# A decoder trunk in float32: the routed experts take their tokens in tiles of 96 in place of 128

## The reference

```
def swiglu(h, w1, w3, w2):
    return (jax.nn.silu(h @ w1) * (h @ w3)) @ w2

def moe_ffn(h, w_router, w1, w3, w2):
    logits = (h @ w_router).astype(jnp.float32)
    top_v, top_i = lax.top_k(logits, TOP_K)
    top_w = jax.nn.softmax(top_v, axis=-1)
    gate = jnp.sum(jax.nn.one_hot(top_i, N_EXPERTS, dtype=jnp.float32) * top_w[..., None], axis=-2).astype(h.dtype)
    y = jnp.zeros_like(h)
    for e in range(N_EXPERTS):
        y = y + gate[..., e:e + 1] * swiglu(h, w1[e], w3[e], w2[e])
    return y
```

## Time and profile before

| | |
|---|---|
| median of 3 runs | 1988.61 us (1986.09 to 1989.08) |
| profiled execution: its time | 1987.18 us |
| profiled execution: span of the core | 1985.4 us |
| TensorE busy | 1911.2 us (96%) |
| VectorE busy | 1471.9 us (74%) |
| ScalarE busy | 1150.4 us (58%) |
| read from memory | 530.83 MB |
| first and last large matmul of the experts start at | 951.35 and 1965.30 us |

### The profile page before, as it was taken

One profiled execution on the slowest core, in us unless ns is written; L12 is line 12 of the kernel. 1 busy time (PEld: TensorE's weight loads), 2 busy tenths in 40 slices (PEclk: granted clock), 3 DMA queues, 4 the chain that ended last, 5 costly groups with the idle time before them and its releaser, 6 DMA issues.

```text
span 1985.4 us, 29859 instructions
## 1 busy us (share of the span) xinstructions
PE 1911.2 (96%) x10960; PEld 1582.2 (80%) x10960; DVE 1471.9 (74%) x1503; ACT 1150.4 (58%) x1245; POOL 93.4 (5%) x134
## 2 busy tenths in 40 slices
PE   5999999999999999998999999999999999999996
PEld 4878888789987888887887787877878878778885
DVE  3755565744567655656788889888888888888888
ACT  2554554334435545542667767677677676767773
POOL 0610100000005201000000000000000000000000
PEclk9999999999999999998999999999999999999998
DMA  8846434685557544344899999999999999999993
GB/s 315 303 151 220 167 127 160 209 315 191 186 179 245 208 140 162 125 161 144 319 342 350 349 344 348 351 339 353 334 353 348 342 345 336 357 341 348 343 364 127
DMA packets 275638, 533.10 MB, mean 269 GB/s; under 512 B 10768, under 2 KB 23392, under 8 KB 275424
## 3 DMA queue, kind: packets, MB, share of 16 engines
q1 hardware_dynamic: 275552, 531.91, 75.6%
HBM read 530.83 MB, written 1.05 MB: 268 GB/s over the span
## 4 chain that ended last, share of the span: by engine, by line
PE 89%; DVE 6%; ACT 2%; issue 1%; DMA 1%; DVEq 1%; SPq 0%; ACTq 0%
PE pA L741 18%; PE pA L742 17%; PE pA L743 17%; PE pA L746 8%; PE pO L746 7%; PE pO L741 6%; PE pO L743 6%; PE pO L742 6%; PE pT L799 4%; DVE w_lo L1846 1%; ACT w_hi L1429 1%; DMA raw<-in_ffn_w 1%; PE pT L746 1%; DVE win L2083 0%; DMA x<-in_x 0%
## 5 line engine op out<-in xcount | busy, mean ns | idle before, releaser
L1891 DVE TENSOR_TENSOR wide_lo<-raw,wide_hi 128x2048 fp32r<-128x2048 f32 x336 | 761.9, 2291 | 122.0 <-ACT wide_hi L1429 102.5
L1429 ACT ACTIVATE wide_hi<-raw 128x2048 fp32r<-128x2048 f32 x336 | 644.8, 1922 | 213.1 <-PE pO L743 119.1
L1429 ACT ACTIVATE w_hi<-raw 128x1024 fp32r<-128x1024 f32 (+1 forms) x242 | 251.2, 1045 | 337.2 <-PE pA L743 234.2
L1846 DVE TENSOR_TENSOR w_lo<-raw,w_hi 128x1024 fp32r<-128x1024 f32 (+1 forms) x242 | 294.4, 1230 | 169.0 <-ACT w_hi L1429 159.9
L741 PE MATMUL pA<-wide_hi,x_lo 128*128 128x512 f32 x896 | 359.7, 401 | 1.8 <-DVE wide_lo L1891 0.6
L743 PE MATMUL pA<-wide_hi,x_hi 128*128 128x512 f32 x896 | 353.5, 395 | 0.0
L742 PE MATMUL pA<-wide_lo,x_hi 128*128 128x512 f32 x896 | 353.5, 395 | 0.0
L741 PE MATMUL pA<-w_hi,h_lo 128*128 128x512 f32 (+2 forms) x560 | 225.8, 403 | 14.7 <-DVE w_lo L1846 10.8
L742 PE MATMUL pA<-w_lo,h_hi 128*128 128x512 f32 (+2 forms) x560 | 216.7, 387 | 0.0
L743 PE MATMUL pA<-w_hi,h_hi 128*128 128x512 f32 (+2 forms) x560 | 216.6, 387 | 0.0
L741 PEld LDWEIGHTS pA<-wide_hi,x_lo 128*128 128x128 f32 x896 | 168.0, 188 | 44.7 <-issue 4.1
(11 more groups left out here) (272 smaller groups left out, 2367.9 us busy)
## 6 DMA issues: line engine op xcount, KB each, us to landing
raw<-in_moe_w SPq DMA_DIRECT2D x336, 1024.0 KB, 6.9
raw<-in_w_in SPq DMA_DIRECT2D x56, 1024.0 KB, 6.0
raw<-in_ada_w SPq DMA_DIRECT2D x48, 1024.0 KB, 6.4
raw<-in_ffn_w SPq DMA_DIRECT2D x33, 1024.0 KB, 5.0
raw<-in_w_out SPq DMA_DIRECT2D x8, 1024.0 KB, 5.0
raw<-in_cmp_k_w SPq DMA_DIRECT2D x4, 1024.0 KB, 8.2
raw<-in_cmp_v_w SPq DMA_DIRECT2D x4, 1024.0 KB, 11.6
raw<-in_w_read_nsa SPq DMA_DIRECT2D x4, 1024.0 KB, 6.0
```

Of the source, the lines that this page charges most:

```text
L1429: return nc.scalar.activation(dst, src, ACT.Copy)
L1846: V.tensor_tensor(w_lo[m][:, 0:n], raw[s][:, i * n:(i + 1) * n], w_hi[m][:, 0:n].bitcast(F32), ALU.subtract).then_inc(raw_done, 1)
L1891: V.tensor_tensor(wide_lo[m][:, :], raw[g][:, :], wide_hi[m][:, :].bitcast(F32), ALU.subtract).then_inc(raw_done, 2)
```

## The change

The experts' tokens are taken in tiles of CAP = 96 places, and there may be PASSES = 3 passes in place of 2, chosen by two comparisons in place of one. sel, x_f, x_hi, x_lo, aT_hi and aT_lo are 96 wide. The outputs of gate_up and down, a_sb and oe use 96 partitions; their 512 columns stay. The streamed weights, their splits and their transfers stay as they are within a pass. The part of SyncE's program that issues an expert pass stands there three times, the second and third under a condition.

```
...
+
+
+CAP = 96
+PASSES = -(-SEQ // CAP)
...
-        aT_hi = sb("aT_hi", [P, CK, SEQ], F32R, at=work)
-        aT_lo = sb("aT_lo", [P, CK, SEQ], F32R, at=work + 4096)
-        x_f = sb("x_f", [P, KB, P], at=work + 8192)
-        x_hi = sb("x_hi", [P, KB, P], F32R, at=work + 12288)
-        x_lo = sb("x_lo", [P, KB, P], F32R, at=work + 16384)
+        aT_hi = sb("aT_hi", [P, CK, CAP], F32R, at=work)
+        aT_lo = sb("aT_lo", [P, CK, CAP], F32R, at=work + 4096)
+        x_f = sb("x_f", [P, KB, CAP], at=work + 8192)
+        x_hi = sb("x_hi", [P, KB, CAP], F32R, at=work + 12288)
+        x_lo = sb("x_lo", [P, KB, CAP], F32R, at=work + 16384)
...
-        sel = sb("sel", [P, TT, P], at=work + 20480)
+        sel = sb("sel", [P, TT, CAP], at=work + 20480)
...
-        slot16 = sb("slot16", [P, TT, 2 * NE + 1])
-        gate16 = sb("gate16", [P, TT, 2 * NE])
+        slot16 = sb("slot16", [P, TT, PASSES * NE + 1])
+        gate16 = sb("gate16", [P, TT, PASSES * NE])
...
-                    passes = sp.value_load(flag[0:1, 0:1], min_val=1, max_val=2)
-                    with sp.If(passes > 1):
-                        experts()
+                    passes = sp.value_load(flag[0:1, 0:1], min_val=1, max_val=PASSES)
+                    for p in range(1, PASSES):
+                        with sp.If(passes > p):
+                            experts()
...
                                 for t in range(TT):
-                                    ins = mm(pA[1 + 2 * q][:, j * P:(j + 1) * P], y[:, t, k * P:(k + 1) * P], sel[:, t, :], t == 0, t == 1)
+                                    ins = mm(pA[1 + 2 * q][:, j * P:j * P + CAP], y[:, t, k * P:(k + 1) * P], sel[:, t, :], t == 0, t == 1)
...
-                                ins = mm3(dst, x_hi[:, at, :], x_lo[:, at, :], wh[:, k * W:(k + 1) * W], wl[:, k * W:(k + 1) * W],
+                                ins = mm3(dst[0:CAP, :], x_hi[:, at, :], x_lo[:, at, :], wh[:, k * W:(k + 1) * W], wl[:, k * W:(k + 1) * W],
...
                         for q in range(2):
-                            turned([a_sb[:, 0, (2 * q + j) * P:(2 * q + j + 1) * P] for j in range(2)], P)
+                            turned([a_sb[0:CAP, 0, (2 * q + j) * P:(2 * q + j + 1) * P] for j in range(2)], P)
...
-                                    ins = mm3(outs[half][:, :], aT_hi[:, k, 0:P], aT_lo[:, k, 0:P],
+                                    ins = mm3(outs[half][0:CAP, :], aT_hi[:, k, :], aT_lo[:, k, :],
...
-                                mm(dst[:, :], selT[:, t * P:(t + 1) * P], oe_lo[:, at], True, False)
-                                mm(dst[:, :], selT[:, t * P:(t + 1) * P], oe_hi[:, at], False, True).then_inc(gather_full if t else T_full, 1)
+                                mm(dst[:, :], selT[0:CAP, t * P:(t + 1) * P], oe_lo[0:CAP, at], True, False)
+                                mm(dst[:, :], selT[0:CAP, t * P:(t + 1) * P], oe_hi[0:CAP, at], False, True).then_inc(gather_full if t else T_full, 1)
...
                     def keep_sel():
...
-                            T_copy(lambda pt: (selT[:, t * P:(t + 1) * P], pt[:, 0:P]))
+                            T_copy(lambda pt: (selT[0:CAP, t * P:(t + 1) * P], pt[0:CAP, 0:P]))
...
                     def silu():
...
-                        nc.scalar.activation(a_sb[:, 0, :], pA[0][:, :], ACT.Silu).then_inc(g_free, 1)
+                        nc.scalar.activation(a_sb[0:CAP, 0, :], pA[0][0:CAP, :], ACT.Silu).then_inc(g_free, 1)
...
                     def hi_a():
...
-                            copy(aT_hi[:, 2 * q:2 * q + 2, 0:P], pt[:, 0:SEQ].rearrange("p (k n) -> p k n", k=2)).then_inc(aT_hi_ready, 1)
+                            copy(aT_hi[:, 2 * q:2 * q + 2, :], pt[:, 0:SEQ].rearrange("p (k n) -> p k n", k=2)[:, :, 0:CAP]).then_inc(aT_hi_ready, 1)
...
-                            copy(oe_hi[:, half * W:(half + 1) * W], pO[b.O.slot(v)][:, :]).then_inc(oe_hi_ready, 1)
+                            copy(oe_hi[0:CAP, half * W:(half + 1) * W], pO[b.O.slot(v)][0:CAP, :]).then_inc(oe_hi_ready, 1)
...
-                    for i in range(2):
+                    for i in range(PASSES):
...
-                    link(V.tensor_scalar(r(9)[:, 1:2], r(9)[:, 0:1], float(P), 1.0, ALU.is_gt, ALU.add))
-                    V.tensor_copy(flag[:, 0:1], r(9)[:, 1:2])
-                    V.tensor_scalar(slot16[:, :, 0:NE], te(8), -1.0, None, ALU.add)
-                    V.tensor_scalar(slot16[:, :, NE:2 * NE], te(8), -1.0 - P, None, ALU.add)
+                    V.tensor_scalar(r(9)[:, 1:2], r(9)[:, 0:1], float(CAP), 1.0, ALU.is_gt, ALU.add)
+                    link(V.tensor_scalar(r(9)[:, 2:3], r(9)[:, 0:1], float(2 * CAP), None, ALU.is_gt))
+                    link(V.tensor_tensor(r(9)[:, 3:4], r(9)[:, 1:2], r(9)[:, 2:3], ALU.add))
+                    V.tensor_copy(flag[:, 0:1], r(9)[:, 3:4])
+                    for i in range(PASSES):
+                        V.tensor_scalar(slot16[:, :, i * NE:(i + 1) * NE], te(8), -1.0 - i * CAP, None, ALU.add)
...
-                    passes = dve.value_load(flag[0:1, 0:1], min_val=1, max_val=2)
+                    passes = dve.value_load(flag[0:1, 0:1], min_val=1, max_val=PASSES)
...
                     def one_hot(e):
...
-                            ins = V.tensor_scalar(sel[:, t, :], iota, slot16[:, t, bass.ds(e, 1)], None, ALU.is_equal)
+                            ins = V.tensor_scalar(sel[:, t, :], iota[:, 0:CAP], slot16[:, t, bass.ds(e, 1)], None, ALU.is_equal)
...
-                                ins = V.tensor_scalar(x_f[:, k, :], pA[1 + 2 * q][:, j * P:(j + 1) * P], mod[:, l, 32 + k:33 + k],
+                                ins = V.tensor_scalar(x_f[:, k, :], pA[1 + 2 * q][:, j * P:j * P + CAP], mod[:, l, 32 + k:33 + k],
...
-                        V.tensor_tensor(a_sb[:, 0, :], a_sb[:, 0, :], pA[2][:, :], ALU.mult).then_inc(a_ready, 1)
+                        V.tensor_tensor(a_sb[0:CAP, 0, :], a_sb[0:CAP, 0, :], pA[2][0:CAP, :], ALU.mult).then_inc(a_ready, 1)
...
-                            V.tensor_tensor(aT_lo[:, 2 * q:2 * q + 2, 0:P], pt[:, 0:SEQ].rearrange("p (k n) -> p k n", k=2),
-                                            aT_hi[:, 2 * q:2 * q + 2, 0:P].bitcast(F32), ALU.subtract).then_inc(free, 1)
+                            V.tensor_tensor(aT_lo[:, 2 * q:2 * q + 2, :], pt[:, 0:SEQ].rearrange("p (k n) -> p k n", k=2)[:, :, 0:CAP],
+                                            aT_hi[:, 2 * q:2 * q + 2, :].bitcast(F32), ALU.subtract).then_inc(free, 1)
...
-                            V.tensor_tensor(oe_lo[:, at], po[:, :], oe_hi[:, at].bitcast(F32), ALU.subtract).then_inc(free, 1)
+                            V.tensor_tensor(oe_lo[0:CAP, at], po[0:CAP, :], oe_hi[0:CAP, at].bitcast(F32), ALU.subtract).then_inc(free, 1)
...
```

More of the change, by code:

```diff
@@ L1254, in _ @@
                     pe.wait_ge(slots_ready, 1)
-                    passes = pe.value_load(flag[0:1, 0:1], min_val=1, max_val=2)
+                    passes = pe.value_load(flag[0:1, 0:1], min_val=1, max_val=PASSES)
                     evacuated(b.A, A_free, 4)
@@ L1750, in _ @@
                     act.wait_ge(slots_ready, 1)
-                    passes = act.value_load(flag[0:1, 0:1], min_val=1, max_val=2)
+                    passes = act.value_load(flag[0:1, 0:1], min_val=1, max_val=PASSES)
                     G, gv = Turn(start=FFB + 1), Turn()
@@ L2506, in last_scattered @@
                             plink(V.tensor_tensor(x[:, t, cols_], x[:, t, cols_], tmp[:, :], ALU.add))
[L2507 removed]
+                            ins = V.tensor_tensor_reduce(x_f.rearrange("p k n -> p (k n)")[:, 0:W], x[:, t, cols_], x[:, t, cols_], 1.0, 0.0,
                                                         ALU.mult, ALU.add, sq[:, t, half:half + 1])
```

3 lines of the change are left out of this document (1 added, 2 removed).

## The result

| | before | after |
|---|---|---|
| median of 5 runs | 1987.38 us (1986.09 to 1989.08) | 1975.56 us (1973.35 to 1978.51) |
| ratio | | 0.9939, 95% interval 0.9925 to 0.9954 |
| profiled execution: its time, its span | 1987.18, 1985.4 us | 1973.35, 1971.6 us |

The changed kernel is 11.8 us faster by the medians and 13.8 us by the two profiled executions (the profiled one of after is the fastest of its five). The forecast was 6.4 us.

The account below looks back on a forecast made before the run. TensorE's own sequence was taken to bound the kernel, not memory. Transposes -5.1, the stand at x_lo -1.1 and the ends -0.2 sum to -6.4 us: 1982.2 us, ratio 0.9968, range 1977.5 to 1988.

Parts of the forecast that it names:

- One pass, the same 336 loads: Expert weights: the largest expert has 75 tokens, under 96, so the changed kernel runs one pass with the same 336 issues.
- The transposes, the main term: Transposes of a_sb (turn_a) stream 96 columns, not 128: 109 to 83 ns each, 196 x 26 ns = 5.1 us saved.
- 49 groups: Groups of four a_sb transposes whose saving counts: 56 less the 7 behind scatters inside the expert loop.
- Behind the scatters nothing is gained: In the block behind each of seven scatters, the 104 ns saved on transposes turn into waiting for wide_lo.
- Gathers at nothing: Gathers stream 96, not 128, but the full 128-column load sets the pace: 0 taken, 6.7 us if they followed the transposes.
- The stand at x_lo, 1.1 us: TensorE stands 0.32 us at each next expert; a shorter x_lo saves 0.15 us, seven times: 1.1 us, bounds 0 and 2.2.
- The ends, -0.2: Start: +0.4 us routing operations, some -0.4 shorter x_f, x_hi, x_lo; end: -0.2 for the last block's aT_hi and aT_lo.
- I take 0: Large expert products with 96 loaded columns: no change in step, bounds 26 ns less to 78 ns more each.
- Rivals: Nothing measurable, 1987.3 us, chance 0.23; slower, 2303, 0.03; second pass, about 3000, 0.02; load on the path, 1884, 0.02.
- The load is on the path after all: Rival for the large products: the shorter stationary load saves 4032 x 26 ns = 105 us, giving 1884; chance 0.02.

Follow-up runs that it names:

- the aligned kernel: The kernel before with every SBUF area of tiles begun on a multiple of 256 bytes, only addresses changed: 1967.42 us, ratio 0.9898.
- the first bench: Model left out: groups of 24 products by loaded width, one bfloat16 group, then transposes, with other engines idle or busy; 96 columns packed took 232.9 ns.
- the bench: Model left out: TensorE alone runs the products' sequence at the kernels' addresses, by width and spacing; 64 columns 384 bytes apart took 232.9 ns.
- The third bench: Model left out: groups of 28 products read one fixed pair of tiles, the start of one tile moved; 226.8 ns with 128 columns, both aligned.

## Why the prediction came out as it did

- **One pass, the same 336 loads**: held.
- **The transposes, the main term**: held. 82 ns where 83 were forecast; alone they gave 4 us, in the sum 5.4 with the shorter step of the product behind them, where 5.1 were forecast. The count of 49 groups is right by luck: it took off seven scatters, and what really drops out is six of them and the last block of all, whose turn_a waits for its own result.
- **Behind the scatters nothing is gained**: held, 0.62 to 0.66 us, and the wait for wide_lo is now marked in the row. It is six of the seven; behind the last one nothing waited before or after.
- **Gathers at nothing**: held; later in the experts nearly all their steps are 111 to 112 ns before and after.
- **The stand at x_lo, 1.1 us**: the stand shrank from 0.32 to 0.22, not to 0.17, 0.7 us in all.
- **The ends, -0.2**: about so. The first large product starts 0.26 us later (951.61, before 951.35), but kernels with the same start have it at 952.8 and 953.1, so 0.26 cannot be read; from the last one to the end of the span 0.3 us are saved.
- **"I take 0" for the 4032 large products**: this is the step that failed. I saw that no row had 96 columns with 512 streamed, gave bounds of -26 and +78 ns, named it the largest unknown at 4.0 us a nanosecond, and then priced it by the nearest row, the record of a transposition with 64 or 128 stationary columns. A record's length is not a step, and that row streams 128 columns, not 512; read as steps the two transpositions agree as well (109.8 and 108.7 ns), so it was the row that did not carry over, and where the operands lie was not asked at all. The term measured -1.9 ns, 7.4 us, the whole of what the forecast lacks of the profiled executions' 13.8: -6.4 - 7.4 = -13.8. The runs show two terms in it: fewer loaded columns at the addresses of before, -3.9 ns a product, and the packing of the tiles at 384 bytes, which the forecast did not price either, +2 ns. The range left it out although the bound on it was written down; a single nanosecond either way would have been 4 us, so an honest range for an unpriced term of 4032 had to be wider than 4.7 us below the forecast.
- **Rivals.** None came in. "The load is on the path after all" is nearest by its sign, and it is not what happens: loads of 134 and 161 ns in the same layout both step 231, and the aligned kernel with loads of 188 ns steps 227.8.

The Trainium skill's rule that loads of other than 128 columns lose a fast mode (TensorE: Matmul & The Clock Gate, "Weight-path perf modes — Fast Weight Load (FWL) and DoubleRow") was weighed ahead and set aside. The trace agrees: the 162 ns of a 96-column load lie on the line of 0.81 ns a column between the 136 and 188 ns of the earlier trace rows, with no jump, and the step of the large products got shorter by the change and not longer.

The Trainium skill says on the same page, under "Step-by-step: what each phase is for", that the stationary load and the stream have SBUF read ports of their own, so that the load takes no bandwidth from the running matmul. The runs here agree for the length of the load and differ for its place: with the distance of the two starts the step moves between 226.7 and 234.3 ns. The Trainium skill's gap (same page, "Back-to-back issue gap") of 512/2.4 + 2.5 = 216 ns came for bfloat16 (215.8 in the first bench); no group of float32r products of 512 columns came under 226.6.

**Open.** Why the distance counts, and why the order differs between the widths, the runs do not say; a conflict of the two reads in the memory would fit, but it was only argued. What makes a sequence of products settle, and which of two patterns it takes, was not settled either, nor why 64 columns 384 bytes apart step 1.6 ns longer in the bench than in the kernel. The third bench tried distances of 32, 96 and 224 once for each width that it had there: 226.7 ns with 96 columns at 224, 226.6 with 64 columns at 96, 234.3 with 128 columns at 96. A distance of 160 was not tried by itself. Every step of the benches comes from one execution each.

## What to carry to other kernels

Where one instruction runs thousands of times back to back, a nanosecond of its step is a term of its own; read the step, start to start, and not the record's length, and where no row shows the new shape, keep its bound in the range. When the shape of a tile changes, its address and spacing change too, and an experiment that changes one and holds the other tells which of them paid. Here the part that helped most, fewer loaded columns, was right only for an accidental placement: laying both operands of float32r matmuls on multiples of 256 bytes gave more than the change (1967.42 against 1975.56 us) with none of it, and so did the change with its tiles 512 bytes apart (1966.85). Neither placement is a rule for every shape: the alignment that took 4 to 6 ns off a product of 512 columns put 2.8 ns on one of 256.

## What the hardware showed that was not expected

- The step of float32r products with 512 streamed columns is not one number: 226.6 to 234.3 ns at a granted clock of 1.00, by the distance of stationary and streamed start modulo 256 bytes, by the number of loaded columns and, at some places, by what ran before. The other engines and the transfers made no difference.
- Such products run in repeating patterns: 226, 227, 227 ns with 128 columns at distance 0, in most groups only after ten steps of 224 to 236 ns.
- Float32 products of 256 columns with 128 loaded went the other way by the same alignment, from 117.0 to 119.8 ns.
- Fewer loaded columns are not faster in themselves: at distance 0 it is 226.7 with 128 and 230.0 with 96 columns, at distance 64 it is 233.3 and 228.4.
- Float32 transposes step by their streamed columns, 109.2, 82.3 and 69.1 ns for 128, 96 and 80; at 64 columns (63.1 ns) they fall behind this.
